# Score products of small head pairs placed between transposes and V products, and masked corners kept in the bias tables

## The chip, the cores and the metric

The kernel runs on one core of a Trainium2 chip. The core has a matrix engine (PE), a vector engine (DVE), a scalar engine (ACT), a general engine (POOL) and a queue engine (SP) that issues most of the DMAs. The metric is the device time of one execution in microseconds (us); the median of three runs counts. Lower is better.

## The reference

One step of a streaming encoder layer is computed for a prompt of 1024 rows and for a decode group of 64 rows with 512 past rows. After a modulated RMS norm and one input projection, two attentions run. Branch A selects, for each query, the 256 keys with the highest indexer scores (a quarter of the keys in decode) and attends to those. Branch B attends to its own chunk of 64 rows and the two before it, with a learned sink per head. A query reads all keys of its own chunk and of earlier chunks, never of a later one. Both add a relative bias from one table.

```python
score = jnp.where(admissible[None], score, NEG)        # k chunk <= q chunk
_, sel = lax.top_k(score, k_sel)
...
logits = jnp.where(valid[:, :, None, None, :], logits, NEG)
probs = jax.nn.softmax(logits, axis=-1)
...
vis = (k_pos[..., None, :] >= 0) & (kch <= qch) & (qch - kch <= W_CHUNKS)
logits = jnp.where(vis[..., None, None, :, :], logits, NEG)
...
merged = jax.nn.sigmoid(p['g_a']) * o_a + jax.nn.sigmoid(p['g_b']) * o_b
return x + gate * (merged @ w_out)
```

## The kernel before

The program is written engine by engine, and each engine runs its list in order; semaphores tie them together. It has three parts. The first (0 to about 557 us) projects the input in pieces, with the selection of keys beside it on DVE. The second (557 to about 809 us) is the attention. The third is the output projections.

The 1024 prompt rows are eight tiles of 128 rows, tiles 0 to 7, and the decode rows are tile 8 (`SAMPLE`). A unit is one head of one branch of one tile: 136 units, numbered tile by tile, in each tile the eight heads of branch A, then the eight of branch B (decode packs two heads in a unit and has four and four). A unit of branch A has 128 keys in tile 0, 256 in tile 1, up to 1024 in tile 7, and 576 in decode; one of branch B has 128, then 256, and 192 in decode. One branch of one tile is a group `g` (2 * tile + branch), and `GEND[g]` is the number of the unit behind its last one.

All engines walk the same loop over steps `s`, one unit a step. PE does, for units `u` and `u + 1` at an even step `s = u`, the score products S (line 1912): three products for each unit, high and low halves of q and k. For branch A it adds the mask product (line 1919), which adds 1e30 where a key isn't selected; in tiles 0 and 1 all admissible keys are selected, and the mask holds only the corner of 64 rows by 64 keys of the next chunk. DVE adds the bias table (`BTA`, `BTB`, `BT0` for tile 0) and takes the minimum into `NM` (line 1588; signs are turned, so that a masked key has a large positive value), ACT takes the exponential (line 1298) into `PB`. PE transposes `PB` (T, line 1851): a pair of units with at most 256 keys together at step `u + 4`, larger units singly at `u + 3`. DVE or ACT copies the transposed blocks from PSUM to `PT` (line 598, 603). PE then takes the V products (V, line 1941) for the pair at step `u + 5`, an odd step. S of a pair waits until DVE's minima of the pair before last are done (`scores_free`), or of all units before it where the pair or the one before has over 512 keys.

After a group's last V, DVE multiplies the result by the gate in `ATS` (line 1571, step `GEND + 4`), which was loaded from `gz`; the first V of the next group waits for that (`att_done`). SP stores the reciprocals of the denominators (line 841), loads them back broadcast (`RB`, line 849), POOL multiplies (line 1048), SP stores the result to `attd` (line 869), and the next gate load into the same half of `ATS` (line 836) waits for that store.

Beside this, `NORM_AT` has POOL prepare the heads of the next tiles (`XX`, from the `QKV` load), and PE transposes them (line 1868). The bias tables lie in DRAM (`btad`, `btbd`) and are loaded in parts. At step 6 DVE fills the two corners of `BTB` and makes the decode tables `IDP` (a packed identity for the mask product), `SINKP` and `NSINKP`. The first loads into `BT0` come in the last chunk of the projection, at pieces `j == 9` of SP's list. The gate pieces are stored through three buffers `STG` (line 745).

## Time and profile before

| | us |
|---|---|
| median of three runs | 1012.96 |
| lowest, highest | 1012.35, 1014.83 |
| the profiled execution | 1011.71 |
| its span, first to last instruction | 1009.9 |

The profile is of one execution. The 1.8 us between its span and its time lie around the program; a difference in the span is a difference in the time. The profiled execution is 1.25 us faster than the median. Matmuls overlap in the pipeline, so that a row's start matters more than its duration: from the start of one group of products to the start of the next is the time that it held PE.

### The profile page before, as it was taken

What the parts mean: (1) busy time and instruction counts of PE and PEld (TensorE: products, weight loads), DVE (VectorE), ACT (ScalarE), POOL (GpSimd) and SP (SyncE); (2) the same over time, 40 slices, a digit from 0 to 9 for tenths busy, and PEclk for the clock granted to TensorE, in tenths of its full rate; (3) what the DMA queues carried; (4) which work ended last, traced back from release to release, by engine and by line L of the source; (5) the groups of instructions that cost most, each with busy time, mean ns of one, the idle gap of its engine ahead of it and who ended that gap; (6) DMA issues with size and microseconds to landing.
All of it is one profiled execution on the core that took longest, in us unless ns stands there. A gap on an engine that the chain in (4) does not pass through costs nothing. (4 is left out here: it accounts for less than half of the span.)

```text
span 1009.9 us, 17430 instructions
## 1 busy us (share of the span) xinstructions
PE 934.0 (92%) x6448; PEld 830.3 (82%) x6462; DVE 654.0 (65%) x1384; ACT 391.8 (39%) x1171; POOL 306.1 (30%) x306
## 2 busy tenths in 40 slices
PE   4859999999999999999999788899889699999998
PEld 2548887888889999999999456667667599999998
DVE  6563366999999999999971456665666663331121
ACT  5674566454422322121211446666555532212100
POOL 0261123222243522122221133323210135536332
PEclk9989999999999999999999679999999899999999
DMA  9820013743452323232142834333316655524342
GB/s 328 300 78 19 25 54 97 227 157 106 154 200 66 115 77 113 76 104 78 55 143 72 246 97 134 118 104 108 101 40 168 193 145 180 166 70 150 116 131 74
DMA packets 110922, 125.86 MB, mean 125 GB/s; under 512 B 10985, under 2 KB 88169, under 8 KB 110714
## 3 DMA queue, kind: packets, MB, share of 16 engines
q1 hardware_dynamic: 100434, 113.77, 35.9%
q10 hardware_dynamic: 10408, 11.01, 3.6%
q8 instruction: 52, 0.85, 0.4%
q14 instruction: 28, 0.23, 0.1%
HBM read 94.96 MB, written 35.75 MB: 129 GB/s over the span
## 5 line engine op out<-in xcount | busy, mean ns | idle before, releaser
L1663 PE MATMUL PS<-HH,WH 128*128 128x384 f32 (+1 forms) x576 | 188.9, 328 | 0.0
L1665 PE MATMUL PS<-HH,WL 128*128 128x384 f32 (+1 forms) x576 | 187.9, 326 | 0.0
L1664 PE MATMUL PS<-HL,WH 128*128 128x384 f32 (+1 forms) x576 | 187.7, 326 | 0.0
L1485 DVE MAX8 M<-SC 128x8 f32<-128x384 f32 (+3 forms) x210 | 175.2, 874 | 11.7 <-DVE SC L1490 11.0
L1490 DVE MATCH_REPLACE8 SC<-M,SC 128x384 f32<-128x384 f32 (+3 forms) x210 | 180.4, 869 | 0.0
L949 POOL TENSOR_TENSOR WL<-RAW,WH 128x512 fp32r<-128x512 f32 x72 | 93.9, 1308 | 159.4 <-ACT WH L1091 159.4
L1663 PEld LDWEIGHTS PS<-HH,WH 128*128 128x128 f32 x576 | 108.1, 188 | 3.7 <-issue 3.7
L1663 PE MATMUL PS<-WH,HH 128*128 128x512 f32 (+2 forms) x264 | 100.2, 380 | 8.7 <-DVE HL L1429 8.7
L1664 PEld LDWEIGHTS PS<-HL,WH 128*128 128x128 f32 x576 | 108.1, 188 | 0.0
L1665 PEld LDWEIGHTS PS<-HH,WL 128*128 128x128 f32 x576 | 108.1, 188 | 0.0
L1298 ACT ACTIVATE PB<-PB,NM 128x256 f32<-128x256 f32 (+9 forms) x136 | 86.3, 635 | 35.5 <-DVE NM L1588 34.9
L1664 PE MATMUL PS<-WL,HH 128*128 128x512 f32 (+2 forms) x264 | 98.8, 374 | 0.0
L1665 PE MATMUL PS<-WH,HL 128*128 128x512 f32 (+2 forms) x264 | 98.8, 374 | 0.0
L1225 ACT ACTIVATE STG<-PS 128x384 f32<-128x384 f32 (+1 forms) x48 | 22.7, 473 | 153.9 <-PE PS L1665 153.9
L1588 DVE CUSTOM_DVE_ANT_0 PB<-PS,BTA 128x256 f32<-128x256 f32 (+6 forms) x56 | 45.8, 820 | 41.7 <-PE PS L1919 24.8
L1663 PE MATMUL PS<-UH,MH 128*128 128x256 f32 x256 | 72.6, 283 | 0.0
L1664 PE MATMUL PS<-UL,MH 128*128 128x256 f32 x256 | 72.5, 283 | 0.0
L1665 PE MATMUL PS<-UH,ML 128*128 128x256 f32 x256 | 72.3, 282 | 0.0
L1851 PE MATMUL PS<-IDF,PB 128*128 128x128 f32 (+1 forms) x436 | 67.5, 291 | 1.4 <-ACT PT L603 1.0
L1663 PEld LDWEIGHTS PS<-WH,HH 128*128 128x128 f32 (+1 forms) x264 | 50.6, 192 | 17.7 <-POOL WL L949 8.5
L1663 PE MATMUL PS<-ZH,WOH 128*128 128x384 f32 (+1 forms) x192 | 62.8, 327 | 1.9 <-POOL WOL L1058 1.9
L1665 PE MATMUL PS<-ZH,WOL 128*128 128x384 f32 (+1 forms) x192 | 62.6, 326 | 0.0
(224 smaller groups left out, 1791.1 us busy)
## 6 DMA issues: line engine op xcount, KB each, us to landing
RAW<-in_w_all SPq DMA_DIRECT2D x72, 256.0 KB, 2.7
gz<-STG SPq DMA_DIRECT2D x48, 192.0 KB, 1.9
WADA<-in_w_ada SPq DMA_DIRECT2D x16, 512.0 KB, 11.9
snat<-STG SPq DMA_DIRECT2D x24, 256.0 KB, 2.0
QKV<-snat SPq DMA_DIRECT2D x8, 768.0 KB, 4.9
GT<-gz SPq DMA_DIRECT2D x32, 192.0 KB, 2.5
XN<-in_x_prompt SPq DMA_DIRECT2D x8, 512.0 KB, 5.9
btad<-bvd ACTq DMA_DIRECT2D x4, 1024.0 KB
```

Source lines behind the costliest of these rows:

```text
L949: nc.gpsimd.tensor_tensor(WL[c % 2][:, k, 0:cw], raw, WH[c % 2][:, k, 0:cw].bitcast(F32), ALU.subtract).then_inc(lo_done, 1)
L1225: nc.scalar.activation(STG[:, q % 3, 0:gn], bank(pbank(p))[:, 0:gn], ACT.Sigmoid).then_inc(piece_ev, 1)
L1298: nc.scalar.activation(PB[u % NPB][0:r, 0:nk], PB[u % NPB][0:r, 0:nk], ACT.Exp, scale=-1.0, bias=NM[0:r, br, h:h + 1], accum_out=DEN[0:r, ...
L1485: V.max(M8[0:r, a, :], w).then_inc(sel_step, 1)
L1490: V.match_replace(w, M8[0:r, a, :], w, TAKEN).then_inc(sel_step, 1)
L1588: V.tensor_tensor_reduce(out=PB[u % NPB][0:r, 0:nk], in0=v, in1=bias, scale=1.0, scalar=init, op0=ALU.add, op1=ALU.min, accum_out=NM[0:r, ...
L1663: T.matmul(out, wh, mh, start=first, stop=False)
L1664: T.matmul(out, wh, ml, start=False, stop=False)
L1665: return T.matmul(out, wl, mh, start=False, stop=last)
L1851: last = T.transpose(out[0:m, c:c + r], PB[v % NPB][0:r, 128 * b:128 * b + m], IDF[0:r, 0:r])
```

## The change

Five edits, all in the attention and what leads to it.

1. The score products become a function `score_pair`. A pair is `alone` when it, or the pair before it, has over 512 keys; such a pair stays at its even step. All others, 45 of 68 pairs, are issued one step earlier, at the odd step, ahead of that step's transposes and V products.
2. In tiles 0 and 1 the mask products of branch A are gone.
3. The corner values stand in the tables in DRAM instead: POOL fills a tile `CORNER`, SP stores it into one corner of `btad` and two of `btbd` at piece `j == 4` of the last chunk, once the tables are complete, and waits for these stores at `j == 9`, before the first table load. DVE's two fills of `BTB` are gone.
4. `IDP`, `SINKP` and `NSINKP` lie elsewhere and are made by DVE before the selection of the decode tile; the wait for the `BTB` load moves from step 6 to step 8 on DVE.
5. SP waits for the last sink sum before the first gate load of the output part, since this load now overwrites the decode tables.

```diff
+                if c == NCH - 1 and j == 4:
+                    sp.wait_ge(bias_out, 16 * 5)
+                    sp.wait_ge(corner_set, 1)
+                    sp.dma_start(btad[0:CHUNK, :, 960:1024], CORNER[0:CHUNK, :, :]).then_inc(corner_out, 16)
+                    sp.dma_start(btbd[0:CHUNK, :, 192:256], CORNER[0:CHUNK, :, :]).then_inc(corner_out, 16)
+                    sp.dma_start(btbd[CHUNK:128, :, 0:64], CORNER[CHUNK:128, :, :]).then_inc(corner_out, 16)
                 if c == NCH - 1 and j == 9:
-                    sp.wait_ge(bias_out, 16 * 5)
+                    sp.wait_ge(corner_out, 48)
...
                 if s == NU + 1:
                     sp.wait_ge(exp_done, NU)
+                    sp.wait_ge(sink_sum, NT)
                     g_load(0)
...
             pool.wait_ge(wgate_pe, GK)
+            nc.gpsimd.memset(CORNER[:], NEG_BIG).then_inc(corner_set, 1)
...
+            dve.wait_ge(gated_out, 64)
+            V.memset(IDP[DEC:128, :, :], 0.0)
+            for i in range(2):
+                V.tensor_copy(IDP[0:DEC, i, :], IDF[0:DEC, 0:DEC])
+                half = slice(DEC * i, DEC * (i + 1))
+                V.tensor_copy(SINKP[half, :], SINK[half, :].rearrange("p (a b) -> p a b", b=2)[:, :, i])
+                link(V.tensor_scalar(NSINKP[half, :], SINK[half, :].rearrange("p (a b) -> p a b", b=2)[:, :, i], -1.0, None, ALU.mult))
             pick_rounds((SAMPLE,), KSEL_S // 8, 3)
...
-                if s == 6:
+                if s == 8:
                     dve.wait_ge(kvb_in, 32)
...
-                    V.memset(BTB[0:CHUNK, :, 192:256], NEG_BIG)
-                    link(V.memset(BTB[CHUNK:128, :, 0:64], NEG_BIG))
...
+            def score_pair(first):
+
+                tt, br, h = UNITS[first]
...
+                if scores_free(first) > 0:
+                    pe.wait_ge(min_done, scores_free(first))
...
+                for u in (first, first + 1):
+                    if br == 0 and tt >= 2:
...
+            def alone(u):
+
+                return max(unit_keys(u), unit_keys(u - 2) if u >= 2 else 0) > 512
...
-                if 0 <= s < NU and s % 2 == 0:
...
+                if 0 <= s < NU and s % 2 == 0 and alone(s):
+                    score_pair(s)
+                if 0 <= s + 1 < NU and s % 2 and not alone(s + 1):
+                    score_pair(s + 1)
                 for x in TP[s]:
```

The rows below are instructions of PE in program order. KT and QT are keys and queries (S), MASK the mask product, PB the probabilities being transposed (T), PT the transposed ones with values VA or VB (V), XX heads of the next tile being transposed. The first place is on PE at the start of tile 1 in the loop, from the scores of units 18 and 19 on. The kernel before:

```order
L1912 MATMUL PS<-KT_143,QT1_145 128x256 x6
L1919 MATMUL PS<-MASK_67,IDB_105 128x256 x2
L1851 MATMUL PS<-IDF_103,PB4_166 128x128
L1851 MATMUL PS<-IDF_103,PB0_162 128x128
L1860 MATMUL PS<-IDF_103,RDEN_129 8x128
L1941 MATMUL PS<-PT1_172,VB_158 64x128 x2
L1912 MATMUL PS<-KT_143,QT1_145 128x256 x6
L1919 MATMUL PS<-MASK_67,IDB_105 128x256 x2
L1851 MATMUL PS<-IDF_103,PB1_163 128x128 x2
L1851 MATMUL PS<-IDF_103,PB2_164 128x128 x2
L1941 MATMUL PS<-PT2_173,VA_156 64x128 x4
```

And the same place on PE in the changed kernel, where lines have moved (S is 1911, T 1860, V 1960):

```order
L1860 MATMUL PS<-IDF_103,PB4_167 128x128
L1860 MATMUL PS<-IDF_103,PB0_163 128x128
L1911 MATMUL PS<-KT_143,QT1_145 128x256 x6
L1869 MATMUL PS<-IDF_103,RDEN_129 8x128
L1960 MATMUL PS<-PT1_173,VB_159 64x128 x2
L1860 MATMUL PS<-IDF_103,PB1_164 128x128 x2
L1860 MATMUL PS<-IDF_103,PB2_165 128x128 x2
L1911 MATMUL PS<-KT_143,QT1_145 128x256 x6
L1960 MATMUL PS<-PT2_174,VA_157 64x128 x4
```

S of the next pair now stands between the transposes and the V products of the same pair, and the mask product is gone.

The second place is the end of branch B of tile 4 on PE, where the next tile's scores have 768 keys. Changed kernel:

```order
L1960 MATMUL PS<-PT0_172,VB_159 64x128 x4
L1860 MATMUL PS<-IDF_103,PB4_167 128x128 x2
L1860 MATMUL PS<-IDF_103,PB0_163 128x128 x2
L1960 MATMUL PS<-PT1_173,VB_159 64x128 x4
L1911 MATMUL PS<-KT_143,QT1_145 128x512 x6
L1911 MATMUL PS<-KT_143,QT1_145 128x256 x6
L1918 MATMUL PS<-MASK_67,IDB_105 128x512
L1918 MATMUL PS<-MASK_67,IDB_105 128x256
L1918 MATMUL PS<-MASK_67,IDB_105 128x512
L1918 MATMUL PS<-MASK_67,IDB_105 128x256
L1860 MATMUL PS<-IDF_103,PB1_164 128x128 x2
L1860 MATMUL PS<-IDF_103,PB2_165 128x128 x2
```

Here the large scores stay at the even step, ahead of the transposes, and transposes and V products of one pair still stand side by side.

On DVE the decode tables now stand ahead of the selection for the decode tile (before, these rows stood at step 6 of the attention loop, followed by the two fills of `BTB`):

```order
L1541 MEMSET IDP_149 64x64
L1543 CAST IDP_149<-IDF_103 64x64
L1545 COPY SINKP_150<-SINK_107 64x4
L1546 TENSOR_SCALAR NSINKP_151<-SINK_107 64x4
L1543 CAST IDP_149<-IDF_103 64x64
L1545 COPY SINKP_150<-SINK_107 64x4
L1546 TENSOR_SCALAR NSINKP_151<-SINK_107 64x4
```

The two corner fills are gone from DVE, and the other seven instructions stand ahead of the loop; what they compute is the same.

## Rows read from the trace of the kernel before

**Rows 1.** The page: PE's busy time and share; granted clock in 40 slices, tenths.
```profile
PE 934.0 (92%) x6448; PEld 830.3 (82%) x6462; DVE 654.0 (65%) x1384; ACT 391.8 (39%) x1171; POOL 306.1 (30%) x306
...
PEclk9989999999999999999999679999999899999999
```

**Rows 2.** Windows: length, PE, PEld, DVE, ACT, POOL busy, clock, DMA share, GB/s.
```profile
574.54:587.45 12.91, 10.76 (x57) 6.61 (x57) 7.88 (x26) 5.43 (x21) 6.88 (x6) 0.50 0.46 130
...
600.64:612.55 11.91, 9.19 (x84) 6.43 (x85) 8.49 (x29) 7.10 (x22) 1.27 (x1) 1.00 0.42 118
```

**Rows 3.** Groups of instructions, 575 to 649: busy, mean ns | idle before, releaser.
```profile
L1912 PE MATMUL PS<-KT,QT 64*128 64x256 f32 (+3 forms) x144 | 19.2, 378 | 0.0
...
L1941 PE MATMUL PS<-PT,VA 128*64 128x128 f32 x144 | 11.4, 295 | 3.7 <-DVE PT L598 1.2 <-ACT PT L598 1.0 <-ACT PT L603 0.7
...
L1941 PE MATMUL PS<-PT,VB 128*64 128x128 f32 x83 | 8.5, 313 | 6.6 <-DVE PT L598 3.7 <-ACT PT L598 2.6 <-issue 0.3
```

**Rows 4.** Windows of one microsecond, columns as in rows 2.
```profile
561.00:562.00 1.00, 0.66 (x2) 0.27 (x2) 0.50 (x3) 1.00 (x6) 0.00 (x0) 0.50 1.02 426
...
594.00:595.00 1.00, 1.00 (x6) 0.81 (x4) 0.44 (x3) 0.60 (x2) 0.92 (x1) 0.50 0.85 241
595.00:596.00 1.00, 0.62 (x9) 0.42 (x8) 1.00 (x4) 0.42 (x2) 1.00 (x3) 0.98 0.08 21
...
793.00:794.00 1.00, 0.49 (x6) 0.49 (x8) 1.00 (x2) 1.00 (x3) 0.00 (x0) 0.50 1.12 326
```

**Rows 5.** Timeline of PE: start, duration, instruction, idle before and its releaser.
```profile
577.83 1.01 PE L1912 MATMUL PS<-KT,QT 64*128 64x256 f32 x6
578.77 0.61 PE L1919 MATMUL PS<-MASK,IDB 128*128 128x256 bf16 x2
579.18 0.63 PE L1851 MATMUL PS<-IDF,PB 128*128 128x128 f32 x2
...
587.45 1.12 PE L1941 MATMUL PS<-PT,VA 128*64 128x128 f32 x8 [0.78 <-DVE PT L598]
...
591.68 1.12 PE L1941 MATMUL PS<-PT,VA 128*64 128x128 f32 x8 [0.77 <-ACT PT L598]
...
600.64 0.66 PE L1941 MATMUL PS<-PT,VB 128*64 128x128 f32 x8 [0.25 <-ACT PT L598]
601.23 0.62 PE L1912 MATMUL PS<-KT,QT 64*128 64x256 f32 x6
...
603.75 0.66 PE L1941 MATMUL PS<-PT,VB 128*64 128x128 f32 x8 [1.31 <-DVE PT L598]
```

**Rows 6.** Timeline of DVE, SP's queue and PE, 564 to 576.
```profile
564.79 0.19 DVE L1550 CAST IDP<-IDF 64x64 bf16<-64x64 f32 x1 [2.45 <-DMA VB<-snat]
...
566.32 0.48 DVE L1556 MEMSET BTB<- 64x512 f32 x1
...
570.25 0.44 SPq L836 DMA_DIRECT2D ATS<-gz  x1
...
573.70 0.69 DVE L1571 TENSOR_TENSOR ATS<-PS,ATS 128x512 f32<-128x512 f32 x1 [2.84 <-DMA ATS<-gz]
...
575.16 0.91 PE L1912 MATMUL PS<-KT,QT 64*128 64x128 f32 x6
```

**Rows 7.** Timeline of PE in a later tile, tile 4 branch B.
```profile
678.06 0.66 PE L1941 MATMUL PS<-PT,VB 128*64 128x128 f32 x8 [0.28 <-issue]
```

**Rows 8.** Timeline of SP's queue: stores of attention results, and a gate load.
```profile
582.67 0.39 SPq L869 DMA_DIRECT2D attd<-ATS  x1
...
593.24 0.37 SPq L869 DMA_DIRECT2D attd<-ATS  x1
595.54 0.36 SPq L836 DMA_DIRECT2D ATS<-gz  x1
...
606.78 0.36 SPq L869 DMA_DIRECT2D attd<-ATS  x1
```

**Rows 9.** Timeline of DVE after the selection for the decode tile.
```profile
536.50 0.42 DVE L575 TENSOR_TENSOR KT<-PS,KT 128x256 fp32r<-128x256 f32 x1 [8.96 <-ACT KT L568]
```

More of the change, by code:

```diff
@@ L173, in build_program @@
         BTBP = at("BTBP", [128, 4, WIN + DEC], F32, 121856)
-        IDP = at("IDP", [128, 2, DEC], BF16, 66560)
-        SINKP = at("SINKP", [128, 4], F32, 66816)
-        NSINKP = at("NSINKP", [128, 4], F32, 66848)
+        IDP = at("IDP", [128, 2, DEC], BF16, XB + 22528)
+        SINKP = at("SINKP", [128, 4], F32, XB + 22784)
+        NSINKP = at("NSINKP", [128, 4], F32, XB + 22816)
+        CORNER = at("CORNER", [128, 8, CHUNK], F32, XB + 18432)
         BT0 = [at("BT0A", [128, 4, 128], F32, WB + 6144), at("BT0B", [128, 4, 128], F32, SCB + 16384)]
@@ L291, in build_program @@
         stg_out = [sem(f"stg_out{i}") for i in range(3)]
+        corner_set = sem("corner_set")
+        corner_out = sem("corner_out")
         kva_in = sem("kva_in")
@@ L1545, in _ @@
                     dve.wait_ge(mask_done, NT)
-                if s == 6:
+                if s == 8:
                     dve.wait_ge(kvb_in, 32)
-                    for i in range(2):
-                        V.tensor_copy(IDP[0:DEC, i, :], IDF[0:DEC, 0:DEC])
-                        half = slice(DEC * i, DEC * (i + 1))
-                        V.tensor_copy(SINKP[half, :], SINK[half, :].rearrange("p (a b) -> p a b", b=2)[:, :, i])
-                        V.tensor_scalar(NSINKP[half, :], SINK[half, :].rearrange("p (a b) -> p a b", b=2)[:, :, i], -1.0, None, ALU.mult)
-                    V.memset(IDP[DEC:128, :, :], 0.0)
-                    V.memset(BTB[0:CHUNK, :, 192:256], NEG_BIG)
-                    link(V.memset(BTB[CHUNK:128, :, 0:64], NEG_BIG))
                 if s == 16:
@@ L1878, in _ @@
                     transposes(TQ[n][1])
+            def score_pair(first):
+                tt, br, h = UNITS[first]
+                nk = unit_keys(first)
+                if h == 0:
+                    wait_evacs(pe, TIDX[("Q", tt, br)])
+                if scores_free(first) > 0:
+                    pe.wait_ge(min_done, scores_free(first))
+                if br == 0:
+                    keys, k0 = (KTAS if tt == SAMPLE else KT[:, 0]), 0
+                else:
+                    keys, k0 = (KTBS, 0) if tt == SAMPLE else (KT[:, 1], 128 * max(tt - 1, 0))
+                last = {}
+                for b in range(0, nk, 512):
+                    m = min(512, nk - b)
+                    for n, (pq, pk) in enumerate(((0, 0), (1, 0), (0, 1))):
+                        for u in (first, first + 1):
+                            half = slice(HD * (u % 2), HD * (u % 2) + HD)
+                            if tt == SAMPLE:
+                                q = QTP[half, pq, 4 * br + 2 * h:4 * br + 2 * h + 2, :].rearrange("p a n -> p (a n)")
+                            else:
+                                q = QT[tt % 2][half, pq, 4 * br + h, :]
+                            last[u] = T.matmul(scores_of(u)[:, b:b + m], q, keys[half, pk, k0 + b:k0 + b + m],
+                                               start=(n == 0), stop=(n == 2 and (br == 1 or tt < 2)))
+                for u in (first, first + 1):
+                    if br == 0 and tt >= 2:
+                        ident = IDP[:].rearrange("p a n -> p (a n)") if tt == SAMPLE else IDB[:]
+                        for b in range(0, nk, 512):
+                            m = min(512, nk - b)
+                            last[u] = T.matmul(scores_of(u)[:, b:b + m], ident, MASK[:, MOFF[tt] + b:MOFF[tt] + b + m], start=False, stop=True)
+                    last[u].then_inc(qk_pe, 1)
+            def alone(u):
+                return max(unit_keys(u), unit_keys(u - 2) if u >= 2 else 0) > 512
             pe.wait_ge(piece_ev, NP)
```

29 lines of the change are left out of this document (removed).

## The prediction

> **What bounds the kernel now.** I read the page first. PE, the matrix engine, is busy 92% of the span, so a gain must come from time in which PE waits, from products that go away, or from PE's clock. The slices of granted clock put the low clock behind the start into the attention part, which begins at 557 us [rows 1]. Second, I cut that part where the first V product of each group starts: 574.54, 587.45, 600.64, 612.55, 623.42, 636.15, 648.83. In the first of these stretches PE is busy 10.76 us of 12.91 at half clock, in the third 9.19 of 11.91 at full clock; DVE is busy 7.88 and 8.49 us [rows 2]. PE is nearest to being the bound, but it doesn't run through. Third, the groups of instructions between 575 and 649: V products sat idle 3.7 and 6.6 us before them, nearly always until DVE or ACT had copied the transposed probabilities, while S products waited 0.0 us [rows 3]. Fourth, the granted clock: 0.50 from 561, still 0.50 at 594, full again from 595, and 0.50 once more at 793, near the end of attention [rows 4].
>
> The pattern in the timeline is the same in each pair of heads: scores S, transposes T of an earlier pair, a wait, V of that same pair. Nothing stands between T and V, so PE waits for the copy out of PSUM: 0.77 us behind ACT, 1.31 us where DVE has something else ahead of its copy [rows 5]. All that follows attention waits for its last products, so time won there should reach the end one for one.
>
> **The change part by part.** I count from the profiled run (span 1009.9 us, 1011.71 as timed) and then set the difference against the median of 1012.96.
>
> *Start of attention, to 574.54: 0.8.* The second V group can't start before DVE has multiplied the first by its gate. DVE waits for the load of ATS until 573.70; SP issues it at 570.25, behind large loads that the change leaves alone [rows 6]. So the mask products of tile 0, and DVE's nine instructions from 564.79 on, two of them the corner fills (0.48 us each, the last to 566.80), are hidden by that load: without them, engines wait longer for it. One thing is left: the scores of the pair that PE takes at 575.16 (0.91 us as a row, some 0.8 net) now run inside the wait.
>
> *The waits, 574.54 to 648.83: 9.5.* In tiles 0 to 3 every pair has at most 512 keys, so the next S stands between T and V. An S holds PE 0.94 us at low clock (577.83 to 578.77) and about 0.6 at full clock [rows 5]. That covers 0.77 at low clock; at full clock some 0.2 stay where nothing else stands there. Of 10.3 us I take 9.5.
>
> *Mask products of tile 1: 1.6.* Four pairs at 0.41 us (578.77 to 579.18) [rows 5].
>
> *The clock: 4.5.* From 574.54 to 595 PE works 10.76 us in the first stretch and 6.8 in the rest (7.55 less the wait of 0.77), less 1.6 of masks: 15.9 us at 0.50 [rows 2, 5]. It came back at 595, after PE had worked from 591.68 on without an idle moment [rows 4, 5]. After the change such stretches begin at 574.5. I let the first 5 us stay low. The other 10.9 shrink by the ratio of one pair at both clocks: 4.23 us less wait 0.77 and mask 0.41, 3.05, low (587.45 to 591.68); 3.11 less 1.31, 1.80, full (600.64 to 603.75) [rows 5]. That is 0.59, so 10.9 become 6.4.
>
> The Trainium skill, "TensorE: Matmul & The Clock Gate", Part 4, says that transposes in PE's transpose mode don't count as busy for the clock gate. By that the clock could stay low as long as before, for T is about a third of each pair; it would take the 4.5 us of this step away, which is the first rival.
>
> *Later tiles: 1.3.* From tile 4 on only the last three pairs of branch B, and the last decode pair, move: 13 of the 45 moved pairs. In four tiles they cover one short wait, 0.28 us (three times, and once 0.49) [rows 7]. The waits behind the next two transposes stay, because the next S there has over 512 keys and isn't moved.
>
> *A limit that isn't PE: -0.5.* Each group passes a chain of transfers: store and broadcast load of its reciprocals, POOL's product, the store of its result, and only then the load of the gate for the group after the next. SP stores the results of group 0 at 582.67 and of group 1 at 593.24, 10.6 us apart, and loads the next gate at 595.54 [rows 8]. PE isn't in this chain. By my sums V starts group 2 (group 1 is the one of 574.5) at 582.3, group 3 at 590.3, group 4 at 600.0, then 610, 621 and 632.3. The load of 595.54 lands 3.4 us later, as the one of 570.25 did, and DVE's product takes 0.7: 599.7, just below 600.0. The next two, each 10.6 later, allow 610.3 and 620.9. So the chain is reached but barely binds: between 0 and 2 us, and I take 0.5.
>
> *Hidden edits: 0.* The decode tables come on DVE ahead of the selection for the decode tile, after which it sat idle for 8.96 us to 536.50, while PE wants the masks at 557; they cost about what the first seven of the nine instructions took from 564.79 on, 0.9 us [rows 6, 9]. The fill of CORNER on POOL lies between the 0.48 of DVE's fill of half such a tile and three times that; POOL waits for a load there. The three stores of corners hold SP's queue for three issues, each at least the 0.4 between two issues and at most 1.1, near 530 us; behind them wait stores of gate pieces, which have three buffers of about 4 us each. Both are below 3.5 us, on engines that have that time. If the cover failed they would cost up to 3.5; they can't gain. SP's added wait before the first gate load of the output part is for a sum that DVE makes before that load is due.
>
> *Sum:* 0.8 + 9.5 + 1.6 + 4.5 + 1.3 - 0.5 = 17.2. DVE, with 8.49 us of work in a stretch that I shorten to 9.7, will be 88% busy [rows 2], and some waits for it will return; I take 1.2 off, an eighth of the waits. Gain 16.0: 1012.96 - 16.0 = 997.0 us (995.7 for the profiled run).
>
> **The rivals.**
> 1. *The clock stays low as long as before, to about 595.* For it: the stretch from 587.45 on had hardly less work in it, and the clock didn't rise. Against: it rose at 595 after a stretch of which a good part was transposes, and it stayed full from 600 to 612 with 9.19 us busy of 11.91 [rows 2, 4]. Gain 16 - 4.5, less 0.5 for waits at the changeover: 1002.
> 2. *The chain of transfers binds.* Between the stores at 593.24 and 606.78 it took 13.5 us before [rows 8]. If that is the chain's own pace, two such groups put the later ones 6 us behind my times. Gain 10: 1003.
> 3. *The waits only move.* V no longer waits for the copy, but T or S waits for DVE, and the clock comes back late. Gain 0.8 + 1.6 + 1.3 and some 3 of the waits: 1006.
> 4. *No change.* Another load holds tiles 1 to 3 at their old times: 1012.
> 5. *Slower.* S now stands in front of V, in tiles 4 to 7 in front of transposes too, and it waits for DVE's minima of the pair before the last. Meanwhile T and V, which could run, stand behind it on PE. It decides from (16 + 3) / 45 = 0.42 us lost in each of the 45 moved pairs: then the kernel is 0.3% slower; at 0.55 it is 24.8 - 16 = 8.8 over, 1022. For it: PE takes its list in order, and DVE is 88% busy in one group. Against: S waited 0.0 us in the small tiles [rows 3], and the minima that it needs come before the product with the gate in DVE's order, so no load stands between.
>
> **How the numbers follow.** Forecast 0.60; rivals 1 to 5: 0.15, 0.10, 0.06, 0.05, 0.04. The forecast's own range is 992.5 (the full 17.2, and a clock that returns at once, 2.1 more, with 1.2 for the rest of its unknowns) to 1000. The whole range takes in rivals 1 and 2 and ends at 1006: 992 to 1006. Faster by over 0.3% (3 us, about what a measurement of this kernel can tell from no change): 0.91; within 0.3%: 0.05; slower: 0.04.
>
> **What the profile after would show.** The first V of the second group still at 574 to 575, with a longer idle time before it. Idle time before V products near 1 us in place of 10.3. The clock full from about 580 in place of 595. The first V of tile 3 branch B near 632 in place of 648.83, and from there a nearly constant distance to before. Stores of attention results 10 to 11 us apart. I am wrong if S or T takes up waits of over 0.3 us a pair, if DVE waits for the gate load in several groups, or if 574.5 itself moves, which would mean that this load isn't what holds it.

## The result and the profile after

The changed kernel took 1005.28 us as the median of five runs (1001.02 to 1005.78), against 1012.35 for the kernel before beside it (1011.74 to 1014.83): a ratio of 0.9912, 95% interval 0.9884 to 0.9940. A second series of six gave 1003.66 (1002.18 to 1007.17) and 0.990 (0.9878 to 0.9922). The forecast was 997.0, in a range of 992 to 1006. So the sign is right and the time lies in the range, but of the 16 us forecast the medians show 7.1 in the first series and 10.2 in the second. The profiled run of after took 1001.29 us with a span of 999.5, 10.4 us under the 1009.9 of before; it is at the fast end of its series, and what can make the others slower comes out below.

First the page, PE's line and the slices of granted clock, against [rows 1]:

```profile
PE 934.9 (94%) x6446; PEld 827.0 (83%) x6446; DVE 651.9 (65%) x1382; ACT 394.1 (39%) x1171; POOL 306.9 (31%) x307
...
PEclk9989999999999999999999779999999899999999
```

PE has the same work (934.9 us, before 934.0) in a shorter span. Next the windows between the first V products of the second, third, fourth and fifth group, with the columns of [rows 2]; the first two of these took 12.91 and 13.19 us before:

```profile
574.26:583.72 9.46, 9.46 (x52) 5.70 (x52) 5.90 (x26) 5.18 (x21) 6.90 (x6) 0.50 0.43 127
583.72:594.29 10.57, 10.57 (x85) 7.55 (x84) 5.62 (x21) 6.30 (x19) 1.27 (x1) 0.78 0.54 159
594.29:605.05 10.76, 10.08 (x87) 6.41 (x86) 9.51 (x28) 7.80 (x24) 6.95 (x6) 1.00 0.30 85
```

PE now works through the first two windows without a gap. But the first is wholly at half clock, and the second still has a mean of 0.78.

The groups of S and V products over the program piece of [rows 3] (here 574 to 638.14, since tile 3's branch B starts 10.7 us sooner):

```profile
L1911 PE MATMUL PS<-KT,QT 64*128 64x256 f32 (+2 forms) x144 | 18.9, 373 | 0.0
L1960 PE MATMUL PS<-PT,VA 128*64 128x128 f32 x144 | 11.4, 297 | 0.0
L1960 PE MATMUL PS<-PT,VB 128*64 128x128 f32 x81 | 8.4, 317 | 3.7 <-DVE ATS L1580 2.9 <-DVE PT L601 0.8
```

Of the 10.3 us of waits behind copies of PT, 0.8 are left. The other 2.9 us are the wait for the gate in front of the whole stretch, whose product on DVE starts at 573.42 (573.70 in [rows 6]). S products wait for nothing, as before.

PE's timeline at that place, and where the clock comes back (compare [rows 5]; the 1.12 us rows are at half clock, the 0.66 us row of the same shape at full clock):

```profile
574.26 0.69 PE L1960 MATMUL PS<-PT,VB 128*64 128x128 f32 x4 [2.88 <-DVE ATS L1580]
...
583.72 1.12 PE L1960 MATMUL PS<-PT,VA 128*64 128x128 f32 x8
...
586.75 1.12 PE L1960 MATMUL PS<-PT,VA 128*64 128x128 f32 x8
587.80 0.91 PE L1860 MATMUL PS<-IDF,PB 128*128 128x128 f32 x4
...
589.56 0.66 PE L1960 MATMUL PS<-PT,VA 128*64 128x128 f32 x8
```

And windows of two microseconds, against [rows 4]: the clock is back at about 588.4, not at 595 as before and not at 580 as forecast.

```profile
586.00:588.00 2.00, 2.00 (x15) 1.45 (x16) 0.93 (x4) 1.99 (x7) 0.00 (x0) 0.50 0.47 133
588.00:590.00 2.00, 2.00 (x20) 1.51 (x19) 1.09 (x3) 0.33 (x2) 0.00 (x0) 0.91 0.23 45
```

In the fourth group one wait for a copy of PT has come back, 0.68 us: DVE's copy stands behind its addition into QT, which itself waited 0.73 us for ACT. Just behind that stands a row that I had not expected: an addition of 128x8 on DVE takes 2.29 us beside a product on POOL, where it takes 0.16 otherwise.

```profile
595.61 0.69 DVE L578 TENSOR_TENSOR QT<-PS,QT 128x512 fp32r<-128x512 f32 x1 [0.73 <-ACT QT L571]
...
596.62 0.69 DVE L601 COPY PT<-PS 128x512 f32<-128x512 f32 x1
...
597.36 0.66 PE L1960 MATMUL PS<-PT,VB 128*64 128x128 f32 x8 [0.68 <-DVE PT L601]
...
598.03 2.33 POOL L1050 TENSOR_TENSOR XX<-XX,RYQ 128x1280 f32<-128x1280 f32 x1
...
598.10 2.29 DVE L1605 TENSOR_TENSOR SD<-NM,SINK 128x8 f32<-128x8 f32 x1
...
643.87 0.16 DVE L1605 TENSOR_TENSOR SD<-NM,SINK 128x8 f32<-128x8 f32 x1
```

In the later tiles the short wait of [rows 7] is gone, and the wait of the next V product has grown (0.86 at 680.72 in before):

```profile
667.33 0.66 PE L1960 MATMUL PS<-PT,VB 128*64 128x128 f32 x8
...
669.81 0.66 PE L1960 MATMUL PS<-PT,VB 128*64 128x128 f32 x8 [1.23 <-DVE PT L601]
```

SP's queue, against [rows 8]: stores of attention results 10.4 us apart, a gate load behind each.

```profile
582.69 0.39 SPq L879 DMA_DIRECT2D attd<-ATS  x1
...
593.12 0.37 SPq L879 DMA_DIRECT2D attd<-ATS  x1
...
595.42 0.36 SPq L846 DMA_DIRECT2D ATS<-gz  x1
...
603.51 0.38 SPq L879 DMA_DIRECT2D attd<-ATS  x1
```

### The profile page after: what moved, and what is told of

Its sections match the earlier page's. It is cut to its first block and busy times, and to the rows that moved or that the text cites. A ratio compares the mean times of both kernels' runs of the same rounds, so it can differ in the third digit from the quotient of the medians.

```text
span 999.5 us, 17414 instructions
## 1 busy us (share of the span) xinstructions
PE 934.9 (94%) x6446; PEld 827.0 (83%) x6446; DVE 651.9 (65%) x1382; ACT 394.1 (39%) x1171; POOL 306.9 (31%) x307
## 5 line engine op out<-in xcount | busy, mean ns | idle before, releaser
L1860 PE MATMUL PS<-IDF,PB 128*128 128x128 f32 (+1 forms) x436 | 69.6, 293 | 1.5 <-ACT PT L606 1.0
L1860 PEld LDWEIGHTS PS<-IDF,PB 128*128 128x128 f32 (+1 forms) x436 | 49.4, 146 | 17.2 <-issue 7.9
```

The source lines that it names most:

```text
L1860: last = T.transpose(out[0:m, c:c + r], PB[v % NPB][0:r, 128 * b:128 * b + m], IDF[0:r, 0:r])
```

## The experiments

Where attention starts differs between profiled runs, by up to 2.6 us (557.0 to 559.6) even among kernels whose work ahead of it is the same. So beside each ratio to the kernel before I use the distance within one trace from the first score product to the first product of the output projection ("attention" in the table). All times are us.

The clock column is the time from which it is full after group 2 has begun; in e9, e10 and e11 there are stretches of full clock before that, told below.

| run | median | ratio, 95% interval | first V of group 2, 3, 4 | clock full from | attention |
|---|---|---|---|---|---|
| before | | | 574.54, 587.45, 600.64 | 595.0 | 251.79 |
| after | 1005.28 | 0.9912 (0.9884 to 0.9940) | 574.26, 583.72, 594.29 | 588.4 | 241.08 |
| e0 after again | 1003.66 | 0.9900 (0.9878 to 0.9922) | 573.66, 584.11, 595.57 | 590.9 | 244.06 |
| e1 order only | 1004.77 | 0.9899 (0.9880 to 0.9919) | 574.97, 586.19, 595.04 | 585.7 | 245.25 |
| e2 tables only | 1013.15 | 0.9996 (0.9981 to 1.0010) | 574.78, 587.49, 602.50 | 600.8 | 254.19 |
| e3 small tiles only | 1002.38 | 0.9893 (0.9871 to 0.9916) | 575.47, 584.92, 594.20 | 585.8 | 240.80 |
| e4 7 wide products | 1002.18 | 0.9882 (0.9863 to 0.9900) | 575.98, 583.43, 593.48 | 576.7 (low again 584 to 587) | 240.62 |
| e5 12 transposes | 999.88 | 0.9866 (0.9848 to 0.9883) | 575.96, 583.15, 592.00 | 577.2 | 237.88 |
| e8 18 half-array products | 1004.36 | 0.9921 (0.9904 to 0.9938) | 579.21, 588.60, 597.45 | 588.5 | 244.26 |
| e6 early gate | 1001.53 | 0.9877 (0.9857 to 0.9896) | 571.19, 580.64, 590.91 | 584.5 | 239.90 |
| e7 POOL split | 1001.75 | 0.9887 (0.9873 to 0.9901) | 574.31, 583.77, 592.91 | 584.4 | 240.47 |
| e9 14 transposes, first | 1000.88 | 0.9895 (0.9873 to 0.9916) | 573.99, 584.46, 594.36 | 587.6 | 241.19 |
| e10 combination | 1001.01 | 0.9894 (0.9876 to 0.9912) | 572.31, 581.79, 592.45 | 586.6 | 238.55 |
| e11 combination, 22 transposes | 999.77 | 0.9868 (0.9850 to 0.9887) | 568.03, 578.33, 589.42 | 584.0 | 239.69 |

### Which part of the change does it

e0 is the kernel after once more.

> The changed kernel once more, unchanged, since its executions fell into two clusters, 1001.0 to 1001.3 and 1005.3 to 1005.8, with mean clocks of 0.974 and 0.969 to 0.971. Theory (the clusters are two return points of the clock in tile 1): the same two clusters; in a profile of the longer one the first V of the second group is still at 574 and the clock comes back some 8 us later than at 588. Rival (a DMA lands later in some executions): in the longer one 574.26 or a store of attention results is some 4 us late, at the same clock.

e1 has only the new order of the score products; masks, tables and stores are as before:

```diff
+                if 0 <= s < NU and s % 2 == 0 and alone(s):
+                    score_pair(s)
+                if 0 <= s + 1 < NU and s % 2 and not alone(s + 1):
+                    score_pair(s + 1)
```

> The kernel before with nothing changed but the place of the score products (45 pairs one step earlier); mask products, corner fills and decode tables as before. Theory (the gain is the covered waits and the clock that comes back earlier): idle time before V products between 574 and 640 under 1.5 us in place of 10.3, gain 7 to 9 us in the span, 1001 to 1004. Rival (the wait of DVE at step 6 and the masks matter): under 5 us of gain.

e2 has everything else of the change, with the scores in the old order:

```diff
-                if 0 <= s < NU and s % 2 == 0 and alone(s):
+                if 0 <= s < NU and s % 2 == 0:
                     score_pair(s)
-                if 0 <= s + 1 < NU and s % 2 and not alone(s + 1):
-                    score_pair(s + 1)
```

> The changed kernel with all score products back at their even steps; corners in the tables, no mask products in tiles 0 and 1, decode tables early. Theory: gain 1.0 to 1.6 us (four mask products of tile 1), V waits as before, 10 us. Rival (the tables' part carries the gain): 5 us or more.

e3 is after with the new order in tiles 0 to 3 alone:

```diff
-                return max(unit_keys(u), unit_keys(u - 2) if u >= 2 else 0) > 512
+                return u >= 64
```

> The changed kernel with only the pairs of tiles 0 to 3 moved; the 13 pairs of branch B in tiles 4 to 8 at their even steps as before. Theory (the move in later tiles only shifts a wait from the first V of branch B to the second, 0.28 us gone and the next from 0.86 to 1.23): the same time as the changed kernel within 0.5 us, the second V of branch B waiting 0.86 us again. My prediction had it 1.3 us slower.

Measured, e0 first. Its six times don't fall into two clusters (1002.18 to 1007.17), and the traced one, 1003.56, is none of the long ones, so neither theory of the clusters was put to the test. But its attention is 3.0 us longer than that of after, and its rows say where: 1.0 us in the second group, 0.9 in the third, where the clock came back 2.5 us later (590.9), and 1.1 in the two groups of tile 7. In the second group a short addition on DVE was again very long, and PE waited for what comes behind it:

```profile
578.27 2.25 DVE L1618 TENSOR_TENSOR DEN<-DEN,ES 128x8 f32<-128x8 f32 x1 [0.24 <-ACT ES L1323]
...
580.90 0.37 PE L1869 MATMUL PS<-IDF,RDEN 128*8 128x128 f32 x1 [0.61 <-DVE RDEN L1627]
```

Then the parts of the change: the order alone gives the whole gain (0.9899 against 0.9912 and 0.9900 for the whole change), the tables alone give none (0.9996, interval 0.9981 to 1.0010). In e2 the waits of V are as before, and its clock came back later still, at 600.8, so the mask products taken out of tile 1 bought nothing that the runs can tell. The later clock can hide a gain: e2's third group took 15.01 us where before took 13.19. Mask products are full-array work too, and the next section shows that such work matters to the clock; whether taking them out delayed it is not shown. And e3 is level with after (0.9893): the moves in tiles 4 to 7 and in the decode pairs are worth nothing. Its rows at the place of [rows 7] say why:

```profile
667.15 0.66 PE L1960 MATMUL PS<-PT,VB 128*64 128x128 f32 x8 [0.28 <-issue]
...
669.81 0.66 PE L1960 MATMUL PS<-PT,VB 128*64 128x128 f32 x8 [0.86 <-DVE PT L601]
```

Without the move the two waits are 0.28 and 0.86, with it 0 and 1.23. The sum stays within 0.1 us: the copy that the second V product needs comes when DVE is done with it, wherever PE spends its time before.

### What brings the clock back

In after PE worked from 574.26 on without a pause and had half clock until 588.4. Three kernels put work that nothing reads into the 2.88 us wait just ahead of it, in a bank that the next transposes overwrite. e4, 7 products of 128x512 bf16:

```diff
+                if s == 13:
+                    q = min(TIDX[x] for z in range(s + 1, S1) for x in TP[z])
+                    wait_evac(pe, q - 3)
+                    for _ in range(7):
+                        T.matmul(bank(4 + q % 3), IDB[:], MASK[:, 0:512], start=True, stop=True)
```

> The kernel after, with 7 more products of 128x512 bf16 that nothing reads (identity by mask table, written into the bank that the next transposes overwrite), in the 2.88 us for which PE stands before the first V product of the second group (574.26). In the kernel after, PE worked without a pause from there and the granted clock still came back only at 588.2, inside tile 1's products. Theory A, that the sort of work decides (many full-array columns bring the clock back, transposes and half-array products do not): the clock is back right behind the 7 products, near 575, the third group's first V product comes near 579.5 and the fourth's near 589.5 instead of 583.72 and 594.29, and the time falls by 4 to 6 us. Theory B, that only the time since PE's last pause decides: PE now works without a pause from 571.4 on, 3 us more, so that the clock comes back 3 us sooner, near 585, and the time falls by 1 to 1.5 us. Theory C, that neither matters there: return between 585 and 591 as in the three runs with this order, no change. If the 7 products take longer than the wait they cost up to 0.5 us at the start of the group.

e5, 12 transposes of 128x128 f32 there:

```diff
+                    for n in range(12):
+                        T.transpose(bank(4 + q % 3)[:, 128 * (n % 4):128 * (n % 4) + 128], IDF[:], IDF[:])
```

> The twin of the run with 7 more products: 12 transposes of 128x128 f32 that nothing reads stand in the same place instead, about as long. Theory A (the sort of work decides): no change, the clock comes back between 585 and 591, the time is that of the kernel after within 1 us. Theory B (the time since the last pause decides): the same as with the 7 products, back near 585, 1 to 1.5 us faster. Both runs together tell A (only the products work) from B (both work alike) and from C (neither).

e8, 18 products of the scores' shape there:

```diff
+                    for n in range(18):
+                        T.matmul(bank(4 + q % 3)[:, 128 * (n % 4):128 * (n % 4) + 128], IDF[0:64, :], IDF[0:64, :], start=True, stop=True)
```

> The third twin of the run with 12 transposes in the wait before 574.26: here 18 products of 64x128 by 64x128 f32, the shape of the scores' products, which use half of the array's rows (6 of them took 0.90 us at a granted clock of 0.50, so about 2.7 us). With 7 products of 128x512 and with 12 transposes of 128x128 the clock came back near 576.5, some 4 us behind the first of them, and not at 585, though the run with the early gate had PE at work without a pause from 561 on and got its clock back only at 584.3. Theory A (what PE works on decides; these two were full-array work, the kernel's own mix of half-array scores and V products is not enough): with half-array products in the same place the clock does not come back near 576.5 but between 584 and 591, and the time is that of the kernel after within 1 us. Theory B (any work in the wait does it): back near 576.5, and 2 to 4 us faster like the twins.

Measured, first PE's timeline in e5 (T rows of one shape fall from 0.69 to 0.44 us):

```profile
572.90 2.82 PE L1947 MATMUL PS<-IDF 128*128 128x128 f32 x12
575.96 0.69 PE L1965 MATMUL PS<-PT,VB 128*64 128x128 f32 x4 [0.24 <-DVE ATS L1580]
576.59 0.69 PE L1860 MATMUL PS<-IDF,PB 128*128 128x128 f32 x2
...
577.96 0.44 PE L1860 MATMUL PS<-IDF,PB 128*128 128x128 f32 x2
```

then in e8, where the 18 products took 7.98 us as 36 rows, not the 2.7 that I had counted:

```profile
571.29 7.98 PE L1947 MATMUL PS<-IDF 64*128 64x128 f32 x36
579.21 0.69 PE L1965 MATMUL PS<-PT,VB 128*64 128x128 f32 x4
...
586.68 1.12 PE L1860 MATMUL PS<-IDF,PB 128*128 128x128 f32 x4
...
589.19 0.66 PE L1860 MATMUL PS<-IDF,PB 128*128 128x128 f32 x4
```

With either kind of full-array work the clock is full by 577.2, in spite of a pause of 0.24 or 0.37 us. With the half-array products it comes back at 588.5, though PE paused nowhere from 561.4 on. So the kind of work decides here and not how long PE has gone without a pause. Each of these is one trace, but the six traces with the new order and no fill at all (after, e0, e1, e3, e6, e7) had their clock back between 584.4 and 590.9. The early-gate run below says the same: no pause from 561.2 to 584.5, half clock all that time. My first theory had transposes on the wrong side: they work as well as wide products. It is shown that these two fills bring the clock back and that e8's doesn't. Which property decides isn't: e8's products use 64 rows of the array, but they are also plain f32 products in two rows each, where e4 has bf16 products and e5 transposes. That the kernel's own mix is weak because of its scores and its V products with 64 columns of output is the likely reading, but no run here changed that mix itself.

What it is worth: e5's attention is 3.2 us shorter than that of after, and 6.2 shorter than e0's. Its interval of the ratio lies below that of the first series of after and overlaps that of the second; of its four times (998.96 to 1001.40) three lie below all eleven of after. From the second group to tile 3's branch B it takes 59.8 us (575.96 to 635.79), after 63.9; the forecast had 57.8. In e4 the clock fell again from 584 to 587, behind V waits of 0.33 and 0.59 us, and the gain was smaller. e8 started its stretch 4.9 us late and was 3.2 late at the fourth group.

### What holds the start of the second group

e6 issues the gate load of the first tile right behind the load of VB:

```diff
+            for i in range(3):
+                sp.wait_ge(stg_out[i], 16 * NST[i])
+            sp.dma_start(ats(0), gz[0:512, tcols(0)].rearrange("(b p) n -> p b n", p=128)).then_inc(zt_in[0], 16)
...
-                if s in ZT_AT:
+                if s in ZT_AT and ZT_AT[s] >= 1:
```

> The kernel after, with the load of the gate's rows for the first tile (ATS, which SP issued at 570.04 behind the loads of VA) issued ahead of the later loads, once the bands' stores have landed. If that load holds the first V product of the second group, as the trace's chain says (PE idle 2.88 us behind DVE's product with ATS, line 1580), that V product starts near 571.4 to 572 instead of 574.26, and the later groups with it: 1 to 2.9 us faster, less what the second group then waits for VA. The rival: VA's load, issued last before it, is next late within 0.5 us, the gain is under 0.5 us. A second rival: the load put ahead delays the bias tables or VA by about its own 3.5 us issue, and the first group starts late, up to 2 us slower.

```profile
570.36 0.90 PE L1914 MATMUL PS<-KT,QT 64*128 64x128 f32 x6
571.19 0.69 PE L1963 MATMUL PS<-PT,VB 128*64 128x128 f32 x4
571.81 0.69 PE L1863 MATMUL PS<-IDF,PB 128*128 128x128 f32 x2
```

The wait of 2.88 us is gone, the group starts at 571.19, and the third group is 3.1 us early as well. So that load did hold 574.26. In the trace attention is 1.2 us shorter than in after: of the rest, 1.3 us went at 640 to 644, where two additions on DVE took 1.22 and 2.15 us, and 0.8 in the last groups. The medians (1001.53 against 1005.28 and 1003.66) agree with a gain of 2 to 4 us; the intervals of the ratios just overlap.

### The slow additions on DVE

e7 cuts POOL's product in five:

```diff
-                    nc.gpsimd.tensor_tensor(x, x, RYQ[0:r, 20 * tt:20 * tt + 20].unsqueeze(2).broadcast_to([r, 20, HD]), ALU.mult).then_inc(xn4_ready, 1)
+                    for h in range(0, 20, 4):
+                        last = nc.gpsimd.tensor_tensor(x[:, h:h + 4, :], x[:, h:h + 4, :], RYQ[0:r, 20 * tt + h:20 * tt + h + 4].unsqueeze(2).broadcast_to([r, 4, HD]), ALU.mult)
+                    last.then_inc(xn4_ready, 1)
```

> The kernel after, with POOL's product of 128x1280 (XX by RYQ, 2.33 us, one for each tile) cut into 5 of 4 heads each, with the same values. In the traces DVE's additions with two operands in SBUF (SD<-NM,SINK) take 0.16 us alone and up to 2.29 us beside that product; in one run the addition at 644.55 took 2.26 us and the eighth group 18.50 us instead of 14.15. If DVE is held for the rest of the POOL instruction that runs when it starts, then no SD addition takes over 0.7 us any more, the V wait of 0.68 us at 597.36 is gone, and the times gather near 1001 with none near 1005.5: the median 2 to 4 us lower than that of the kernel after. The rival, that the two engines slow one another by traffic and not by the instruction: SD additions still reach over 1.5 us and the times still fall in two groups. POOL's 4 added instructions cost it about 0.1 us each beside work that nobody waits for.

The reason for trying it stood in after and in e1. In e1 DVE's addition was caught in the eighth group (its timeline, then windows of five microseconds):

```profile
644.46 2.33 POOL L1039 TENSOR_TENSOR XX<-XX,RYQ 128x1280 f32<-128x1280 f32 x1
...
644.55 2.26 DVE L1596 TENSOR_TENSOR SD<-NM,SINK 128x8 f32<-128x8 f32 x1
...
647.61 0.80 PE L1902 MATMUL PS<-KT,QT 64*128 64x512 f32 x2 [1.80 <-DVE NM L1588]
```

```profile
645.00:650.00 5.00, 3.04 (x21) 2.29 (x22) 2.84 (x5) 1.96 (x6) 3.08 (x2) 0.71 0.15 52
650.00:655.00 5.00, 5.00 (x32) 3.71 (x32) 3.15 (x7) 2.48 (x6) 0.00 (x0) 0.61 0.78 222
```

The addition ends when POOL's product does, the scores wait 1.80 us for the minimum behind it, PE's clock falls, and the group takes 18.5 us where after takes 14.1: 4.4 us from one addition of eight columns. In e7 the V wait of the fourth group and the two additions of the eighth stand beside POOL like this:

```profile
595.98 0.66 PE L1962 MATMUL PS<-PT,VB 128*64 128x128 f32 x8 [0.67 <-DVE PT L601]
...
641.89 1.27 POOL L1045 TENSOR_TENSOR XX<-QKV,GAM 128x512 f32<-128x512 f32 x1
...
642.44 0.74 DVE L1607 TENSOR_TENSOR SD<-NM,SINK 128x8 f32<-128x8 f32 x1
...
643.66 2.90 POOL L1051 TENSOR_TENSOR XX<-XX,RYQ 128x256 f32<-128x256 f32 x5
...
643.91 0.38 DVE L1620 TENSOR_TENSOR DEN<-DEN,ES 128x8 f32<-128x8 f32 x1
```

The first addition ends at 643.18, when POOL's uncut product of 1.27 us does (643.16); the second started in the first of the five parts (0.58 us each) and ended with it, at 644.29. So DVE's addition is held to the end of the POOL instruction that it meets, and the size of that instruction sets the loss: up to 2.29 us beside 2.33 in after, 0.38 beside one of the parts. The Trainium skill, "SBUF — State Buffer", section "SBUF: two separate sides", calls it an exclusive lock for a whole instruction, where DVE has two inputs in SBUF and GpSimd reads SBUF. The traces agree.

What such a hold costs depends on who needs the result. The V wait that I had expected to go with it stayed: 0.67 us in e7 against 0.68 in after, where it stands ahead of the held addition and not behind it. The fourth group took 10.76 us with the addition of 2.29 us (after), 10.70 with one of 0.17 (e0) and 10.71 in e7. A hold of 2.25 or 2.29 us in the second group cost 1.0 (e0, e9), one of 2.1 in the eighth 0.9 (e4), and the one of 2.26 in e1 4.4, since the clock fell with it (647.1 to 653.9).

The times of e7 lie between 1000.39 and 1003.03, while seven of the eleven runs of after lie above that, up to 1007.17. The intervals of the ratios overlap, e5 and e8 have series as narrow with POOL's product uncut, and the start of attention alone moves by up to 2.6 us between executions. So the holds can carry part of the spread of after, as the 1.0 us in e0 shows; that cutting the product narrows it isn't shown, with one trace in each series.

### Can both be had, and what is next late

e9 is after with 14 transposes in the first wait of attention (1.78 us, ahead of the third pair's scores at 560.43):

```diff
+                if s == 3:
+                    q = min(TIDX[x] for z in range(s, S1) for x in TP[z] if TIDX[x] >= EARLY_T)
+                    wait_evac(pe, q - 3)
+                    for n in range(14):
+                        T.transpose(bank(4 + q % 3)[:, 128 * (n % 4):128 * (n % 4) + 128], IDF[:], IDF[:])
```

> The kernel after, with 14 transposes of 128x128 f32 that nothing reads in the 1.78 us wait in front of the third pair's scores (560.43), just before the clock falls at 561.9. Theory A (the full-array work keeps the clock up): no fall at 561.9, V pairs of the first group 1.4 us apart instead of 2.07; but the second group's first V product still waits for the gate's rows (near 574.3), PE then stands for some 6 us, the clock falls there, and the time gains nothing to 1 us. Theory B (the clock falls whatever is put there): as the kernel after in every stage.

The clock stays up, where in after it had fallen at 561.1, and the pairs of the first group are 1.4 us apart, but PE then stands 5.91 us for the gate, the clock falls there, and attention is as long as in after (241.19 against 241.08), and the ratio (0.9895) is near e0's (0.9900): work in front of a load gains nothing.

e10 is e6, e7 and e9 together.

> The kernel after with three edits together: the gate's rows of the first tile loaded early, POOL's product in five parts, and the 14 transposes in the wait at 560.43. If all three readings hold, the clock stays up through the first two groups, the second group's first V product starts near 568 to 571 (571.19 with the early load alone), the third near 575.5 to 578 (580.64), SD additions take under 0.8 us, and the time is 3 to 6 us below that of the early load alone: 995 to 999 us. Next late would be DVE's row minima or the loads of VB and VA. The rival: DVE cannot keep up with a PE at full clock there, waits come back, the clock falls again in the second group, and the time stays within 1 us of the early load alone (1000 to 1002).

The time is that of the rival, its mechanism is not: the clock fell already in the first group, at 566.1, when PE waited 0.97 us for the load of VB and not for DVE, and was back only at 586.6, and the ratio (0.9894) is no better than that of e6 (0.9877).

e11 adds 8 transposes in that wait:

```diff
                 if s == 8:
+                    q = min(TIDX[x] for z in range(s, S1) for x in TP[z] if TIDX[x] >= EARLY_T)
+                    wait_evac(pe, q - 3)
+                    for n in range(8):
+                        T.transpose(bank(4 + q % 3)[:, 128 * (n % 4):128 * (n % 4) + 128], IDF[:], IDF[:])
                     pe.wait_ge(kvb_in, 32)
```

> The combination of the run before (early gate rows, POOL's product in five parts, 14 transposes in the wait at 560), with 8 more transposes in the wait for the load of VB, 0.97 us long there (566.40), behind which the clock fell at 566.4. If the pause brought the fall, the clock now stays up through the first two groups: V pairs 1.4 us apart, the second group's first V product near 571 and the third's near 578.5 (counted with scores starting near 559; 572.31 and 581.79 before), and the time falls by 2 to 4 us against 1001.01: 997 to 999 us. If the kernel's own mix of products loses the clock there whatever fills the pause, it falls again before 571 and the time stays at 1000 to 1002.

Now the clock stays up to 577.2, and the second group starts at 568.03, earlier than I had expected (571). But then DVE stands for the next gate load, and V with it (timelines of SP's queue, DVE and PE). The median, 999.77, is a little above the 997 to 999 that I had put down.

```profile
570.76 0.43 SPq L849 DMA_DIRECT2D ATS<-gz  x1
...
576.64 0.69 DVE L1585 TENSOR_TENSOR ATS<-PS,ATS 128x512 f32<-128x512 f32 x1 [3.43 <-DMA ATS<-gz]
...
578.33 1.12 PE L1974 MATMUL PS<-PT,VA 128*64 128x128 f32 x8 [3.83 <-DVE PT L601]
...
611.69 0.66 PE L1974 MATMUL PS<-PT,VB 128*64 128x128 f32 x8 [1.40 <-DVE ATS L1585]
```

The stores on SP's queue in e11 come when they came in after (582.69, 593.12, 603.51):

```profile
583.26 0.39 SPq L882 DMA_DIRECT2D attd<-ATS  x1
...
593.48 0.37 SPq L882 DMA_DIRECT2D attd<-ATS  x1
...
603.86 0.37 SPq L882 DMA_DIRECT2D attd<-ATS  x1
```

PE was 6.2 us ahead at 568, and no store is earlier than in after, all within 0.6 us of it. The first of these waits for POOL, which starts on the next tile's products when their load has landed, at 575.7 in both kernels, and needs until 583. From there the stores are 10.2 to 10.4 us apart.

Two different things held V. The wait of 3.83 us at 578.33 is not the chain that the forecast described, since no store of attention results stands ahead of this load. SP issued it at 570.76, behind the other loads on its queue, and DVE had its rows 5.9 us later. At 611.69 it is that chain: the gate load behind the store of 603.86 came late, and the group ahead of 611.69 took 11.49 us where it takes 10.0 in after and e5. So the chain of rival 2 is real, but in e11 it cost about 1.5 us, less than the one late load. How far off it is in after can be read: the gate load issued at 596.18 in e11 let DVE's product start at 599.11, 2.9 us later, while in after the load of 595.42 is used only at 603.22, some 5 us after it had landed by that measure. In e5 DVE waited 1.70 us for a gate load once (its product at 623.40), and no V behind it waited. e5 and e11 have the lowest ratios of the study, 0.9866 and 0.9868; e5 is after with twelve transposes more.

## Why the prediction was right in sign and too large

- **What bounds the kernel, and the cover of the waits.** Right. S between T and V took the waits of 10.3 us down to 0.8; the sum had 9.5 us of gain, and e1, with the new order alone, has the gain of the whole change. S itself waited 0.0 us, so rival 5 (slower) had no ground, and rival 3 (waits only move) neither.
- **The start at 574.5.** Right: 574.26, with the longer wait ahead of it (2.88 us against 1.68), and e6 shows that the gate's load was what held it.
- **The clock: the term that was mis-sized.** I let the first 5 us from 574.5 stay low because before the clock had come back after some such stretch of unbroken work. It stayed low for 14.1. That is about 8.9 us more at half clock than forecast (579.5 to 588.4), and at my own ratio of 0.59 it costs 3.6 us. The times show it: the third group is 1.4 us later than forecast (583.72 against 582.3), the fourth 4.0 (594.29 against 590.3). The step that failed is the inference from "no idle moment" to "full clock". e4, e5 and e8 put in its place: what PE works on there. e5, with its clock at full from 577.2, won back 4.1 of the 6.1 us that were missing between the second group and tile 3's branch B; its clock was back 1.2 us after the group's start, where the term had let 5 stay low, so that about 1.6 of the 4.1 lie beyond the term. What the Trainium skill, "TensorE: Matmul & The Clock Gate", Part 4, says of transposes, which I had set beside this step, pointed the right way for the time, but the row goes against it as a reason: twelve transposes brought the clock back.
- **Mask products of tile 1: 1.6.** Not seen. In the trace of after the products are gone, but e1 keeps them and is as fast, and e2 drops them and gains nothing (0.9996). The intervals leave about 1.5 to 2 us open, so even the 1.6 can't be excluded.
- **Later tiles: 1.3.** Wrong. I counted the 0.28 us waits that go and held the next wait to be unchanged. It grew from 0.86 to 1.23. Between the first V of tile 3's branch B and the output part after takes 160.70 us, before 160.44: no gain, and e3 shows the same from the other side.
- **The chain of transfers: -0.5.** Right in size for this kernel. The stores shown are 10.4 us apart, and no V waits for a gate behind 574.26. With the clock back early it is still about right: no V waits for a gate in e5 behind the first 0.24 us, and in e11, which is further ahead, the chain costs about 1.5.
- **Returning waits: -1.2.** About right in sum (0.8 us of V waits) and in who is late, DVE. But DVE wasn't full: in e0, without a hold, it was busy 7.74 us of the 10.70 of the fourth group, 72% and not 88%, and the same wait (0.67) stood there. It comes from the order of DVE's list, in which the copy stands behind an addition that waits for ACT. The fourth group took 10.76 us where I had 9.7: 0.68 of that is this wait, and about 0.5 is work that moved into it, four pairs of scores with 384 keys and masks instead of three and one of 256.
- **Hidden edits: 0.** Nothing in the traces speaks against it. The three stores of corners took 0.6 us each on SP's queue, at 529 to 531 us, and attention starts at 556.9 to 559.6 us with them, at 557.5 (before) and 558.3 (e1) without.
- **The sum.** By the first V of tile 3's branch B: forecast 632.3, measured 638.14. Of these 5.8 us, 4.0 are there by the fourth group (3.6 of them by the clock), 1.1 more come in the fourth group (the wait and the moved work), 0.8 later. The end gained 10.4 us of span. The medians gained less than the profiled run (7.1 and 10.2 us), since about half of the executions of after are 3 to 5 us slower; of the mechanisms seen, a held addition can do that (4.4 us in e1), and a clock that comes back later takes its part (0.9 in e0). Which it was in the slower executions is open.
- **The rivals.** None came out as described. The outcome lies between the forecast and rival 1: the clock back at 588.4, between 580 and 595. Rival 2 became visible only with PE made faster. The median of 1005.28 is near the times of rivals 2 and 3 (1003 and 1006), but the rows show neither. It lies outside the forecast's own range, which ended at 1000, and within the whole range by 0.7 us, only because that range took in the rivals: that much is luck.

## What to carry to other kernels

Before counting on a clock that comes back, look at which stretches it came back in, by the kind of products and not by idle time alone; a handful of full-array transposes in a wait that PE has anyway is a cheap test, and here a cheap gain. A copy that one engine owes to two consumers in turn keeps its date: taking away the first wait makes the second one longer. And price an edit against the chain that runs beside the bound engine: here it had some 5 us to spare, and in e11 one gate load issued late took more of what PE had won than that chain did.

## What the runs showed of the hardware

- Half clock for 23 us of unbroken work of PE on half-array scores, V products of 64 columns and a third of transposes (e6, 561.2 to 584.5), and full clock at 577 behind 2.8 to 3.2 us of full-array products or transposes (e5, e4).
- In e9 and e11 the same mix kept the full clock through the first group once it had it, even over a wait of 0.82 us (e9); in e10 it lost it at a wait of 0.97. After a fall it came back in the new order after 3 (e4) to 31 us (e0), in the old one after 34 (before) and 41 us (e2), the waits in between included. Where exactly it comes back scattered from 584.4 to 590.9 among kernels with the same order there, and I have no row that explains this.
- An f32 addition of 128x8 with both inputs in SBUF took 0.16 us alone and up to 2.29 us when it started beside a POOL product of 2.33 us; beside a part of 0.58 it took 0.38. Such a hold cost the group between 0.06 (after) and 4.4 us (e1). Five parts cost POOL 2.90 us in all.
- A load issued behind others on SP's queue can set the start of a stage: moved ahead of them, the gate load let the second group start at 571.19 instead of 574.26 (e6).
- 18 products of 64x128 by 64x128 f32, at half clock, took 7.98 us in 36 rows, while six score products of that shape in fp32r took 0.90.
